# A decoder layer on one core: the first attention stage moved ahead of the memory's keys and values

## The chip, the core and the metric

The kernel runs on one core of a Trainium2 chip. The metric is device time in microseconds (us) of one execution; lower is better. Before the change the median of three runs is 1987.96 us (1984.94 to 2330.19).

The core has a matrix engine (TensorE, PE in the rows, with its weight loads as PEld), VectorE (DVE), ScalarE (ACT), GpSimd (POOL) and SyncE (SP), which in this kernel only issues DMAs. Each engine runs its own instructions in program order and waits on semaphores for the others.

## What is computed

One layer of a decoder with 1024 tokens of width 1024, all in f32:

```python
h = rmsnorm(x, attn_norm)
proj = h @ w_in
qkv_a, b_q, b_k, b_v, m_q = split(proj)
o_a = dilated_mixture_attn(qkv_a, positions)      # A: 3 groups (dilation 1, 4, 16), 4 heads of 64
o_b = sink_swa_gqa(b_q, b_k, b_v, positions)      # B: window 128, 8 query and 2 key heads
o_m = memory_attn(m_q, mem, w_mem_kv)             # M: 4 heads of 128 into 256 memory tokens
merged = sum(sigmoid(h @ w_gate + b_gate) * (o @ w_o)) over the three branches
x = x + merged @ w_out
x = x + conv_ffn(rmsnorm(x, ffn_norm))            # up, causal conv of 3, SwiGLU, down
```

Queries and keys are normalised per head, and in A and B a quarter of the head's dimensions is rotated by angles made from `positions`. The memory's keys and values are `rmsnorm(mem) @ w_mem_kv`.

## The kernel before

The program is four blocks one after the other: `input_projections` (projections and all attention), `gated_outputs`, `output_projection` and `feed_forward`. Only the first is changed.

A product of two f32 matrices is made from three: every operand is split into a high part (a cast by ACT) and a low part (the rest, a subtraction by POOL or DVE), and PE sums hi*hi, hi*lo and lo*hi.

The work of `input_projections` is a list of stages, `STAGES` (line 26). A stage has eight slices of a weight (128 rows each, 512 or 768 columns) and two or eight tiles of 128 tokens. A job is one tile against all eight slices: 24 matmuls of 512 columns (memk, memv, M), with 24 more of 256 columns in A and B. There is one place for the split weights (`w_hi`, `w_lo`), so slice k of the next stage is cast (`cast_slice`, L571) only when the last job of the stage before it has used its slice k; then it is lowered (`w_low`, L351) by POOL for even and by DVE for odd k. Before the split a slice lies raw in one of a few places, some of them in `attn_out`, which is filled with results only later; `raw_slot` gives the place, and SP loads into a place when the slice that it held has been split.

Before the change the stages run as memk, memv, A0, A1, A2, B, M: jobs 0 and 1 are memk, 2 and 3 memv, 4 to 11 A0 (dilation 1), 12 to 19 A1, and so on.

All engines go through slots j = 0, 1, 2, ... In slot j:

- PE projects job j, slice by slice (`project`, L1027 and L1029). After slice 5 it turns the queries and keys of job j-1 (`turn`, L1051).
- ACT, DVE and POOL make them ready before that: ACT squares the projection (L585) and copies values out (L594, L598), DVE sums the squares (L774), POOL takes the root (L488, L490), DVE scales (L798), POOL multiplies by the gains (L499) and rotates (L510 to L515).
- The attention of job j-2 is done in two or four units between the slices (`score`, `turn_probs`, `weigh_values` on PE, `minima` on DVE, `exps` on ACT).

A token tile is prepared by a chain of its own: load, `x_square` (ACT, L559), `x_rms` (POOL, L472 and L473), `x_scale` (DVE, L702), `turn_x` (PE, eight transposes, L998), `x_gain` (DVE, L709), `x_high` (ACT, L539), `x_low` (POOL or DVE, L339). There are ten tiles: numbers 0 and 1 are of the memory and are prepared first, 2 to 9 are of x. The latter come in pairs in slots 0, 2, 4 and 5 (`X_SLOTS`), each at fixed places among the slot's other instructions. Two PSUM areas are shared by the tiles, the turned queries and the scores, so these wait for each other.

SP's queue, in order: the memory tiles, the gains' rows, four weight slices, x tiles 2 and 3, four more slices; then, when slices are split, the other six x tiles; then `load_constants` (positions in three orders, head gains and sinks, 11 small DMAs); then the slices of memv and of all later stages. The angles are made by DVE in slots 1 (`angles`, L714 to L733) and 4 (`reduce_angles`, L743 to L751), the sines by ACT, and the tables by DVE (L759 to L762).

## Time and profile before

| | us |
|---|---|
| median of three runs (1984.94, 1987.96, 2330.19) | 1987.96 |
| span of the profiled execution, first to last instruction | 1979.5 |
| PE busy | 1859.2 (94%) |
| DVE busy | 710.4 (36%) |
| POOL busy | 581.4 (29%) |
| ACT busy | 539.1 (27%) |
| DMA, 90.75 MB | 15.1% of 16 engines' span |

The profiled execution is known by its span alone; the page gives no device time for it. Its span is 5.4 us below the fastest run and 8.5 us below the median, and that difference is what lies around the first and the last instruction, and what one run differs from another. The page's times are from the span's start. A row gives busy time, count and mean of a group of instructions, and the idle time of their engine just before them with what ended it. The granted clock is a share of TensorE's full 2.4 GHz: 1.00 or 0.50, and in between where a stretch holds both.

### The profile page before, as it was taken

How to read it: one execution, taken by the hardware profiler on the slowest of the kernel's cores; microseconds unless marked ns; L12 is line 12 of the kernel's file. 1: busy time of each engine (PE TensorE's matmuls, PEld its weight loads, DVE VectorE, ACT ScalarE, POOL GpSimd, SP SyncE). 2: the span in 40 equal slices, each digit the busy share in tenths (PEclk: the TensorE clock that was granted, in tenths of full speed). 3: DMA queues.
4: the chain of work that ended last, by engine and by line, in shares of the span. 5: the costliest groups of instructions: out<-in, count | busy, mean ns of one | idle time of the engine just before them, and what ended most of it. 6: DMA issues, size and time to landing. Idle time of an engine off the chain costs nothing. (4 is left out here: it accounts for less than half of the span.)

```text
span 1979.5 us, 23310 instructions
## 1 busy us (share of the span) xinstructions
PE 1859.2 (94%) x8777; PEld 1483.2 (75%) x8777; DVE 710.4 (36%) x1318; ACT 539.1 (27%) x1029; POOL 581.4 (29%) x503
## 2 busy tenths in 40 slices
PE   4799999998877979999999989899999999999999
PEld 3577999986665856666666668688888888888887
DVE  4634223235666431111111153242444243424343
ACT  4434223233344431111111142322122212221221
POOL 5445235343232211111111053242133213321321
PEclk8899999998999989999999999899999999999999
DMA  5202002000010042111110060221122102210102
GB/s 197 83 32 65 1 1 64 1 17 14 2 42 1 1 88 54 45 38 35 38 45 24 0 198 1 64 85 32 32 64 64 41 23 64 64 42 21 43 22 85
DMA packets 112818, 90.75 MB, mean 46 GB/s; under 512 B 16812, under 2 KB 97388, under 8 KB 112748
## 3 DMA queue, kind: packets, MB, share of 16 engines
q1 hardware_dynamic: 112748, 89.81, 15.1%
q8 instruction: 44, 0.72, 0.2%
q14 instruction: 26, 0.21, 0.0%
HBM read 85.54 MB, written 4.26 MB: 45 GB/s over the span
## 5 line engine op out<-in xcount | busy, mean ns | idle before, releaser
L1779 PE MATMUL ps<-act_hi,f_hi 128*128 128x512 f32 x704 | 274.7, 390 | 6.3 <-DVE f_lo L1547 6.3
L1779 PE MATMUL ps<-act_lo,f_hi 128*128 128x512 f32 x704 | 274.6, 390 | 0.0
L1779 PE MATMUL ps<-act_hi,f_lo 128*128 128x512 f32 x704 | 274.5, 390 | 0.0
L1547 POOL TENSOR_TENSOR f_lo<-merged,f_hi 128x1024 fp32r<-128x1024 f32 x65 | 156.6, 2438 | 83.7 <-ACT f_hi L1628 83.7
L1320 PE MATMUL ps<-act_hi,g_hi 128*128 128x512 f32 x384 | 170.5, 444 | 3.2 <-DVE g_lo L1303 3.2
L1027 PE MATMUL ps<-w_hi,act_hi 128*128 128x512 f32 x320 | 160.4, 501 | 8.1 <-DVE attn_out L709 4.8
L1779 PEld LDWEIGHTS ps<-act_hi,f_hi 128*128 128x128 f32 x704 | 132.7, 188 | 34.1 <-DVE f_lo L1547 6.6
L1292 DVE TENSOR_TENSOR gate<-ps,gate 128x512 f32<-128x512 f32 x48 | 33.2, 692 | 345.4 <-PE ps L1330 345.4
L1330 PE MATMUL ps<-attn_out,o_w 128*128 128x512 f32 x320 | 148.3, 602 | 6.8 <-ACT o_w L1244 3.2
L1734 DVE TENSOR_TENSOR attn_out<-ps,attn_out 128x512 f32<-128x512 f32 x160 | 106.1, 686 | 134.6 <-PE ps L1799 134.6
L1779 PEld LDWEIGHTS ps<-act_hi,f_lo 128*128 128x128 f32 x704 | 132.6, 188 | 27.6
L1779 PEld LDWEIGHTS ps<-act_lo,f_hi 128*128 128x128 f32 x704 | 132.6, 188 | 27.6
L1276 POOL TENSOR_TENSOR g_lo<-g_raw,g_hi 128x1024 fp32r<-128x1024 f32 x23 | 54.5, 2370 | 330.3 <-ACT g_hi L1239 330.3
L1320 PE MATMUL ps<-act_lo,g_hi 128*128 128x512 f32 x384 | 150.9, 393 | 0.0
L1320 PE MATMUL ps<-act_hi,g_lo 128*128 128x512 f32 x384 | 150.5, 392 | 0.0
L1027 PE MATMUL ps<-w_lo,act_hi 128*128 128x512 f32 x320 | 144.8, 453 | 0.0
L1027 PE MATMUL ps<-w_hi,act_lo 128*128 128x512 f32 x320 | 144.3, 451 | 0.0
L1799 PE MATMUL ps<-f_hi,z_hi 128*128 128x512 f32 x352 | 137.0, 389 | 0.2 <-issue 0.2
L1799 PE MATMUL ps<-f_hi,z_lo 128*128 128x512 f32 x352 | 136.9, 389 | 0.0
L1799 PE MATMUL ps<-f_lo,z_hi 128*128 128x512 f32 x352 | 136.9, 389 | 0.0
L1256 ACT ACTIVATE gate<-ps,gate_bias 128x512 f32<-128x512 f32 x48 | 33.0, 687 | 324.7 <-PE ps L1320 324.6
L1330 PEld LDWEIGHTS ps<-attn_out,o_w 128*128 128x128 f32 x320 | 58.8, 190 | 72.4 <-issue 67.0
(198 smaller groups left out, 3340.0 us busy)
## 6 DMA issues: line engine op xcount, KB each, us to landing
merged<-in_w_up_dram SPq DMA_DIRECT2D x44, 512.0 KB, 4.0
g_raw<-in_w_gate_dram SPq DMA_DIRECT2D x23, 512.0 KB, 3.9
merged<-in_w_down_dram SPq DMA_DIRECT2D x22, 512.0 KB, 3.5
attn_out<-in_x_dram SPq DMA_DIRECT2D x16, 512.0 KB, 5.0
attn_out<-in_w_in_dram SPq DMA_DIRECT2D x20, 384.0 KB, 4.0
w_raw<-in_w_in_dram SPq DMA_DIRECT2D x12, 384.0 KB, 3.3
w_raw<-in_w_out_dram SPq DMA_DIRECT2D x16, 256.0 KB, 3.7
out_dram<-attn_out SPq DMA_DIRECT2D x8, 512.0 KB, 2.6
```

The costliest lines, as they stand in the source:

```text
L1027: ins = pe.matmul(proj_a(j)[:, 0:na], lhs, w[:, k, 0:na], start=(k == 0 and i == 0), stop=(k == 7 and i == 2))
L1256: act.activation(gate[:, u % 2, :], ps[:, 2 * (u % 3), :], ACT.Sigmoid, bias=bias[:, bass.ds(column, 1)]).then_inc(gate_done, 1)
L1276: pool.tensor_tensor(g_lo[:, b], g_raw[:, b], g_hi[:, b].bitcast(F32), ALU.subtract).then_inc(g_lo_done[b], 1)
L1292: dve.tensor_tensor(gate[:, u % 2, :], ps[:, 2 * (u % 3) + 1, :], gate[:, u % 2, :], ALU.mult).then_inc(weighed, 1)
L1320: ins = pe.matmul(ps[:, 2 * (u % 3), :], w[:, b, k, :], a[:, k, cols], start=(k == 0 and i == 0), stop=(k == NK - 1 and i == 2))
L1330: ins = pe.matmul(ps[:, 2 * (u % 3) + 1, :], o_w[:, O_SLOT[b] + i, :], attn_out[:, t0 + i, cols], start=(i == 0), stop=(i == tiles - 1))
L1547: eng.tensor_tensor(f_lo[:, b, :], f_raw[b], f_hi[:, b, :].bitcast(F32), ALU.subtract).then_inc(f_lo_done[b], 1)
L1734: dve.tensor_tensor(dst, ps[:, 4 + i % 4, :], dst, ALU.add).then_inc(y_added, 1)
L1779: ins = pe.matmul(ps[:, 2 * q + half, :], w[:, q, k * P:(k + 1) * P], a[:, k, half * 512:(half + 1) * 512], start=(k == 0 and i == 0), sto ...
L1799: ins = pe.matmul(ps[:, (0 if last else 4) + i % 4, :], z[:, p, t * P:(t + 1) * P], w[:, 4 + p, half * 512:(half + 1) * 512], start=(p == ...
```

## The change

The stage list begins with A0; memk and memv follow, then A1 as before. So jobs 0 to 7 are now A0, 8 and 9 memk, 10 and 11 memv, and from job 12 on nothing moves. Tiles 0 to 7 are now of x, and 8 and 9 of the memory. Tiles 0 and 1 are prepared first, 2 to 5 among the slices of slot 0, 6 to 9 in slot 1. The order is written out by hand on each engine.

The memory's split tiles move to the space of `attn_out`, over x tiles that are done with. A0's and memk's and memv's raw slices have four places each. `load_constants` now comes after x tile 3 and ahead of A0's raw slice 4. The memory tiles are loaded into the places of x tiles 4 and 5, once the tiles up to 6 (for tile 8) and up to 7 (for tile 9) are split. The angles, their reduction, the sines and the tables are made in slots 0 and 1. DVE makes the angles with two multiplications over 192 columns in place of 16 over 24, for which POOL writes eight frequencies. The squares of x tiles go to a buffer of their own. The space reserved for dynamic DMA descriptors is set to 1024 bytes; it makes room in memory, and POOL issues no DMA here.

```diff
 STAGES = [
+    ("A", 0, 0, 0, 512, 256, 8),
     ("memk", 0, 0, 0, 512, 0, 2),
     ("memv", 0, 0, 512, 512, 0, 2),
-    ("A", 0, 0, 0, 512, 256, 8),
     ("A", 1, 1, 768, 512, 256, 8),
     ("A", 2, 2, 1536, 512, 256, 8),
     ("B", 0, 0, 2304, 512, 256, 8),
...
     if n < 8:
-        first, places = 0, (0, 1, 6, 7, 8, 9, 10, 11)
+        first, places = 0, (0, 1, 2, 3)
     elif n < 24:
-        first, places = 8, (0, 1, 2, 3)
+        first, places = 8, (0, 1, 10, 11)
...
-        x_slot = [attn_out[:, n, :] for n in range(NX)]
+        x_slot = [attn_out[:, 2 + n, :] for n in range(8)] + [attn_out[:, 6 + n, :] for n in range(2)]
...
+        def x_place(n):
+
+            return (act_hi, act_lo, n) if n < 8 else (mem_hi, mem_lo, n - 8)
+
+        def x_group(n):
+            return n if n < 2 else 1 + n // 2
...
+            def load_x(n):
+                sp.dma_start(x_slot[n], x_t[n] if n < 8 else mem_t[n - 8]).then_inc(x_in[x_group(n)], 16)
...
+                if n == 0:
+                    load_x(0)
+                    sp.dma_start(gain_rows[0:NK, :], attn_norm[0].rearrange("(k p) -> k p", p=P)).then_inc(gain_in, 16)
+                    sp.dma_start(gain_rows[NK:2 * NK, :], mem_norm[0].rearrange("(k p) -> k p", p=P)).then_inc(gain_in, 16)
+                if n == 1:
+                    load_x(1)
                 if n == 4:
                     load_x(2)
+                    load_x(3)
+                    load_constants()
+                if n == 6:
+                    load_x(4)
+                    load_x(5)
                 if n == 8:
-                    for m in (4, 6, 8):
-                        w_split(sp, m - 2)
-                        w_split(sp, m - 1)
+                    load_x(6)
+                    load_x(7)
+                    for m in (8, 9):
+                        x_split(sp, m - 1)
                         load_x(m)
-                    load_constants()
+                if n == 8 + 2:
+                    x_split(sp, 8)
...
+            freqs = np.exp(np.arange(HALF, dtype=np.float32) * np.float32(-2.0 * math.log(ROPE_THETA) / ROT))
+            for f in range(HALF):
+                link(pool.memset(freq[:, f:f + 1], float(freqs[f])))
...
+            x_rms(0)
+            x_rms(1)
+            x_low(pool, 0)
+            w_low(pool, 0)
+            w_low(pool, 2)
+            x_rms(2)
+            x_rms(3)
+            w_low(pool, 4)
+            x_low(pool, 2)
+            x_rms(4)
+            x_rms(5)
+            w_low(pool, 6)
+            x_low(pool, 4)
+            x_rms(6)
+            x_rms(7)
...
+                if j == 1:
+                    x_low(pool, 6)
+                    x_rms(8)
+                    x_rms(9)
+                    x_low(pool, 8)
...
+            x_square(0)
+            x_square(1)
+            x_high(0)
+            cast_slice(0)
+            x_high(1)
+            cast_slice(1)
+            cast_slice(2)
+            cast_slice(3)
+            x_square(2)
+            x_square(3)
+            cast_slice(4)
+            cast_slice(5)
+            x_high(2)
+            x_high(3)
+            x_square(4)
+            x_square(5)
+            cast_slice(6)
+            cast_slice(7)
+            x_high(4)
+            x_high(5)
+            x_square(6)
+            x_square(7)
+            sines()
...
+                if j == 1:
+                    x_high(6)
+                    x_high(7)
+                    x_square(8)
+                    x_square(9)
+                    x_high(8)
+                    x_high(9)
...
+                for part in range(2):
+                    link(dve.tensor_tensor(angle[:, part, :].rearrange("p (o f) -> p o f", f=HALF),
+                                           pos_f[:].rearrange("p o t -> p (o t)").unsqueeze(2).to_broadcast([P, 24, HALF]),
+                                           freq[:].unsqueeze(1).to_broadcast([P, 24, HALF]), ALU.mult))
...
+            x_scale(0)
+            x_scale(1)
+            x_gain(0)
+            x_gain(1)
+            w_low(dve, 1)
             x_low(dve, 1)
-            for k in range(1, 8, 2):
-                w_low(dve, k)
-            for n in pair_of(0):
-                x_scale(n)
+            w_low(dve, 3)
+            x_scale(2)
+            x_scale(3)
+            w_low(dve, 5)
+            x_gain(2)
+            angles()
+            x_gain(3)
+            x_scale(4)
+            x_scale(5)
+            w_low(dve, 7)
+            x_gain(4)
+            x_low(dve, 3)
+            x_gain(5)
+            x_low(dve, 5)
+            reduce_angles()
+            x_scale(6)
+            x_scale(7)
             n = 0
             for j in range(NJ + LAG + 1):
                 if 0 <= j - 1 < NJ:
                     sum_squares(j - 1)
+                    if j == 1:
+                        rope_tables()
...
+                if j == 1:
+                    x_gain(6)
+                    x_gain(7)
+                    x_low(dve, 7)
+                    x_scale(8)
+                    x_scale(9)
+                    x_gain(8)
+                    x_gain(9)
+                    x_low(dve, 9)
...
                 if k == 0:
                     if kind in ("memk", "memv"):
-                        x_split(pe, 2)
-                    elif s == 2:
-                        x_split(pe, 3 + t)
+                        x_split(pe, NX)
+                    elif s == 0:
+                        x_split(pe, t + 1)
...
+                    if j == 0 and k % 2:
+                        turn_x(2 + k // 2)
+                    if j == 1 and k < 4:
+                        turn_x(6 + k)
                     if k == TURN_AT[0] and 0 <= j - 1 < NJ:
-                        if j <= X_SLOTS[-1]:
-
-                            pe.wait_ge(x_gained, 1 + 2 * sum(slot <= j for slot in X_SLOTS) + (j not in X_SLOTS))
+                        if j == 1:
+                            pe.wait_ge(x_gained, NX)
                         turn(j - 1, 0)
...
-    nc = _bacc.Bacc("TRN2", target_bir_lowering=False, num_devices=1)
+    nc = _bacc.Bacc("TRN2", target_bir_lowering=False, num_devices=1, dynamic_dma_scratch_size=1024)
```

On SP, before: the queue from the last x tile to memv's first slice. `pos_i` are the positions, `gains` the head gains, `w_raw` a raw slice.

```order
L388 DMA attn_out<-in_x_dram 128x1024
L393 DMA pos_i<-in_positions_dram 128x8x1
L395 DMA pos_i<-in_positions_dram 128x4x1 x2
L397 DMA pos_i<-in_positions_dram 128x8
L400 DMA gains<-in_a_q_norm_dram 128x192
L400 DMA gains<-in_a_k_norm_dram 128x192
L400 DMA gains<-in_b_q_norm_dram 128x64
L400 DMA gains<-in_b_k_norm_dram 128x64
L400 DMA gains<-in_m_q_norm_dram 128x128
L400 DMA gains<-in_m_k_norm_dram 128x128
L401 DMA neg_sink<-in_b_sinks_dram 128x8
L440 DMA w_raw<-in_w_mem_kv_dram 128x512
```

On SP, after: the same queue from the last of the small DMAs on (L391, L392), with A0's raw slices 4 to 7 (L442), the x tiles 4 to 7 and the two memory tiles (L379).

```order
L391 DMA gains<-in_m_k_norm_dram 128x128
L392 DMA neg_sink<-in_b_sinks_dram 128x8
L442 DMA w_raw<-in_w_in_dram 128x768
L442 DMA w_raw<-in_w_in_dram 128x768 [waits w_lo_odd]
L379 DMA attn_out<-in_x_dram 128x1024 [waits w_lo_even]
L379 DMA attn_out<-in_x_dram 128x1024
L442 DMA attn_out<-in_w_in_dram 128x768
L442 DMA attn_out<-in_w_in_dram 128x768 [waits w_lo_odd]
L379 DMA attn_out<-in_x_dram 128x1024 [waits w_lo_even]
L379 DMA attn_out<-in_x_dram 128x1024
L379 DMA attn_out<-in_mem_dram 128x1024 [waits x_lo_odd,x_lo_even] x2
L442 DMA w_raw<-in_w_mem_kv_dram 128x512
```

Before, no weight slice of the first stage stood behind the small DMAs; now the slices 4 to 7 do, and the memory tiles wait for low parts.

On DVE, before: its first instructions, up to the first normalised queries and keys.

```order
L702 TENSOR_SCALAR attn_out<-attn_out,row_rstd 128x1024 [waits x_rstd] x2
L709 TENSOR_TENSOR attn_out<-ps,norm_gain 128x1024 [waits gain_ready,x_turned]
L709 TENSOR_TENSOR attn_out<-ps,norm_gain 128x1024 [waits x_turned]
L339 TENSOR_TENSOR mem_lo<-attn_out,mem_hi 128x8x128 [waits x_hi]
L351 TENSOR_TENSOR w_lo<-w_raw,w_hi 128x512 [waits w_hi_done]
L351 TENSOR_TENSOR w_lo<-attn_out,w_hi 128x512 [waits w_hi_done] x3
L702 TENSOR_SCALAR attn_out<-attn_out,row_rstd 128x1024 [waits x_rstd] x2
L709 TENSOR_TENSOR attn_out<-ps,norm_gain 128x1024 [waits x_turned] x2
L339 TENSOR_TENSOR act_lo<-attn_out,act_hi 128x8x128 [waits x_hi]
L774 TENSOR_REDUCE head_ss<-square 128x4 [waits sq_done]
L798 TENSOR_TENSOR qk<-ps,head_rstd 128x512 [waits rstd_done]
```

On DVE, after: from the low part of slice 3 on, in slot 0 (L347 is `w_low`, L724 `x_scale`, L731 `x_gain`, L335 `x_low`).

```order
L347 TENSOR_TENSOR w_lo<-attn_out,w_hi 128x768 [waits w_hi_done]
L724 TENSOR_SCALAR attn_out<-attn_out,row_rstd 128x1024 [waits x_rstd] x2
L347 TENSOR_TENSOR w_lo<-w_raw,w_hi 128x768 [waits w_hi_done]
L731 TENSOR_TENSOR attn_out<-ps,norm_gain 128x1024 [waits x_turned]
L736 TENSOR_SCALAR neg_sink<-neg_sink 128x8 [waits const_in]
L739 TENSOR_REDUCE parity<-prob 128x1 [waits masks_built,dve_chain]
L740 TENSOR_SCALAR parity<-parity 128x1 [waits dve_chain]
L743 TENSOR_SCALAR masks<-masks,parity 128x64 [waits dve_chain] x2
L749 CAST pos_f<-pos_i 128x24 [waits dve_chain]
L751 TENSOR_TENSOR prob<-pos_f,freq 128x192 [waits dve_chain] x2
L731 TENSOR_TENSOR attn_out<-ps,norm_gain 128x1024 [waits x_turned,dve_chain]
L724 TENSOR_SCALAR attn_out<-attn_out,row_rstd 128x1024 [waits x_rstd] x2
```

Before, all eight slices were lowered ahead of the third tile; now the gains of tiles 2 to 5 stand behind the low parts of slices 5 and 7.

## Rows read from the trace of the kernel before

**Rows 1.** Stretches: busy time of each engine, granted clock, DMA share, GB/s.

```profile
core 0: us, PE busy (x) PEld busy (x) DVE busy (x) ACT busy (x) POOL busy (x), PEclk, DMA share, GB/s
0.00:108.00 108.00, 63.80 (x287) 52.15 (x288) 61.85 (x81) 43.88 (x66) 55.25 (x65) 0.83 0.39 129
108.00:185.00 77.00, 75.13 (x515) 61.05 (x514) 25.78 (x79) 32.15 (x85) 35.54 (x51) 1.00 0.11 37
```

**Rows 2.** Who waited for whom, PE, 0 to 110 us: total, times, longest.

```profile
PE ps L1051 <- POOL qk L499: 9.5, 1, 9.5
```

**Rows 3.** Timeline of ACT: squares after A0's jobs 1 and 7.

```profile
107.73 0.60 ACT L585 ACTIVATE square<-ps 128x512 f32<-128x512 f32 x1 [3.46 <-PE ps L1029]
...
185.94 0.59 ACT L585 ACTIVATE square<-ps 128x512 f32<-128x512 f32 x1
```

**Rows 4.** Timeline of SP, 20 to 36 us, and the first cast behind it.

```profile
20.54 4.17 SPq L388 DMA_DIRECT2D attn_out<-in_x_dram  x6
24.75 0.53 SPq L393 DMA_DIRECT2D pos_i<-in_positions_dram  x1
25.32 4.14 SPq L395 DMA_DIRECT2D pos_i<-in_positions_dram  x2
...
32.01 0.43 SPq L400 DMA_DIRECT2D gains<-in_a_q_norm_dram  x1
...
35.34 0.91 SPq L440 DMA_DIRECT2D w_raw<-in_w_mem_kv_dram  x2
...
43.03 1.29 ACT L571 ACTIVATE w_hi<-w_raw 128x512 fp32r<-128x512 f32 x2 [7.37 <-DMA w_raw<-in_w_mem_kv_dram]
```

**Rows 5.** DMA issues, 0 to 120 us: KB each, median us to landing.

```profile
attn_out<-in_w_in_dram SPq DMA_DIRECT2D x8, 384.0 KB, 4.6
...
attn_out<-in_mem_dram SPq DMA_DIRECT2D x2, 512.0 KB, 4.0
```

**Rows 6.** Timeline, one tile's chain: the first tile.

```profile
6.35 1.05 ACT L559 ACTIVATE square<-attn_out 128x1024 bf16<-128x1024 f32 x1
...
8.43 0.75 DVE L702 TENSOR_SCALAR attn_out<-attn_out,row_rstd 128x1024 f32<-128x1024 f32 x1 [8.43 <-POOL row_rstd L473]
...
11.25 1.23 DVE L709 TENSOR_TENSOR attn_out<-ps,norm_gain 128x1024 f32<-128x1024 f32 x1 [0.59 <-PE ps L998]
...
13.64 2.35 POOL L339 TENSOR_TENSOR mem_lo<-attn_out,mem_hi 128x1024 fp32r<-128x1024 f32 x1 [3.77 <-ACT mem_hi L539]
```

**Rows 7.** Groups by shape, 0 to 110 us: slices of 768 columns, and the cast.

```profile
L351 POOL TENSOR_TENSOR w_lo<-w_raw,w_hi 128x768 fp32r<-128x768 f32 x2 | 3.7, 1851 | 2.0 <-ACT w_hi L571 2.0
L571 ACT ACTIVATE w_hi<-w_raw 128x768 fp32r<-128x768 f32 x4 | 3.3, 838 | 5.7 <-DMA w_raw<-in_w_in_dram 5.7
...
L351 DVE TENSOR_TENSOR w_lo<-attn_out,w_hi 128x768 fp32r<-128x768 f32 x2 | 2.7, 1352 | 1.0 <-ACT w_hi L571 1.0
```

**Rows 8.** Timeline: DVE's small multiplications, its reduction of the angles; one job's POOL chain.

```profile
53.50 3.56 DVE L733 TENSOR_SCALAR prob<-pos_f 128x24 f32<-128x24 f32 x16
...
90.28 0.25 DVE L743 TENSOR_SCALAR prob_t<-prob 128x192 f32<-128x192 f32 x1
...
93.63 0.36 DVE L751 TENSOR_SCALAR prob<-prob 128x384 f32<-128x384 f32 x1
...
96.54 0.20 POOL L488 TENSOR_SCALAR head_rstd<-head_ss 128x8 f32<-128x8 f32 x1 [7.26 <-DVE head_ss L774]
...
102.21 0.45 POOL L515 TENSOR_TENSOR qk<-rope_a,rope_b 128x128 f32<-128x128 f32 x1
```

**Rows 9.** Timeline of PE: two matmuls' starts at the lower clock, two at the full.

```profile
90.40 0.63 PE L1027 MATMUL ps<-w_lo,act_hi 128*128 128x512 f32 x1
...
91.04 0.63 PE L1027 MATMUL ps<-w_hi,act_lo 128*128 128x512 f32 x1
...
92.00 0.39 PE L1027 MATMUL ps<-w_lo,act_hi 128*128 128x512 f32 x1
...
92.35 0.39 PE L1027 MATMUL ps<-w_hi,act_lo 128*128 128x512 f32 x1
```

More of the change, by code:

```diff
@@ L80, in raw_group @@
 def raw_group(n):
-    place = raw_slot(n)
-    if n < 8:
-        return n
-    return place if place < 4 else 2 + place % 4
+    return {0: 0, 1: 1, 2: 2, 3: 3, 4: 2, 6: 3, 8: 6, 9: 7, 10: 4, 11: 5}[raw_slot(n)]
 def raw_before(n):
@@ L163, in layer @@
         half_power = sb("half_power", [P, 16])
+        with ExitStack() as early:
+            sb("below_mem", [P, 2, S], ctx=early)
+            mem_hi = sb("mem_hi", [P, NK, 256], F32R, ctx=early)
+            mem_lo = sb("mem_lo", [P, NK, 256], F32R, ctx=early)
         attn_out = sb("attn_out", [P, 10, S])
@@ L237, in input_projections @@
         stats = sb("stats", [P, 3, 8, 8])
-        with ExitStack() as early:
-            mem_hi = early.enter_context(nc.sbuf_tensor("mem_hi", [P, NK, 256], F32R))
-            mem_lo = early.enter_context(nc.sbuf_tensor("mem_lo", [P, NK, 256], F32R))
         q_ring = sb("q_ring", [P, RQ, 4, P])
@@ L261, in input_projections @@
                  (("max", 32), ("e", 96), ("total", 32), ("f", 96))}
-        mem_in = [sem(f"mem_in{n}") for n in range(2)]
-        x_in = [sem(f"x_in{n}") for n in range(4)]
+        x_in = [sem(f"x_in{n}") for n in range(6)]
         const_in = sem("const_in")
@@ L355, in v_wait @@
         def v_wait(eng, j):
-            before = units_before(j - RK + 2)
+            writer = [i for i in range(j) if KIND[i] in V_KINDS and KIND[i] != "memv" and i % RK == j % RK]
+            before = units_before(writer[-1] + 2) if writer else 0
             if before:
@@ L474, in x_rms @@
                                    ALU.pow).then_inc(x_rstd, 1)
-            for n in (0, 1):
-                x_rms(n)
-            x_low(pool, 0)
             def norm_and_rope(j):
@@ L537, in x_high @@
                 act.wait_ge(x_gained, n + 1)
[L538 removed]
+                hi, _, c = x_place(n)
+                if n == 8:
+                    x_split(act, 4)
                 act.activation(hi[:, :, c * P:(c + 1) * P], x_slot[n].rearrange("p (k n) -> p k n", n=P),
@@ L582, in squares @@
                         act.wait_ge(factor_turned, spreads)
-                    if j <= X_SLOTS[-1]:
-                        act.wait_ge(x_sq, 2 + 2 * sum(slot <= j + 1 for slot in X_SLOTS))
                     ins = act.activation(square[:, 0:512], proj_a(j), ACT.Square)
@@ L654, in _ @@
             act.activation(norm_gain[:].rearrange("p a k -> p (a k)"), ps[:, OB, 0:2 * NK], ACT.Copy).then_inc(gain_ready, 1)
-            for n in (0, 1):
-                x_square(n)
-            for n in (0, 1):
-                x_high(n)
-            for k in range(8):
-                cast_slice(k)
-            for n in pair_of(0):
-                x_square(n)
+            x_square(0)
[21 more added lines that the diff above has]
+            sines()
             n = 0
@@ L666, in _ @@
                     squares(j - 1)
-                for m in pair_of(j + 1):
-                    x_square(m)
+                if j == 1:
[5 more added lines that the diff above has]
+                    x_high(9)
                 for k in range(8):
@@ L674, in _ @@
                         n += 1
-                    if k == 4:
-                        for m in pair_of(j):
-                            x_high(m)
                     if k == TURN_AT[0] and 0 <= j - 1 < NJ:
@@ L971, in _ @@
                         merge_use(MERGE_AT.index((j, k)))
-                if j == 1:
-                    angles()
-                if j == 4:
-                    reduce_angles()
-                    rope_tables()
                 if j == merge_from:
@@ L991, in turn_x @@
                     pe.wait_ge(x_gained, n - 1)
-                    keys = count(HAS_K, slot_of_x(n) - 1)
-                    if keys:
-                        pe.wait_ge(k_done, keys)
                 elif n == 1:
```

69 lines of the change are left out of this document (10 added, 59 removed).

## The prediction

> **What bounds the kernel now.** I read the page first: PE is busy for 1859.2 of 1979.5 us, so the change can win only where PE is idle or runs at the lower clock, in the part that it touches. The stretches come next. In the first 108 us PE is busy for 63.8 us at a granted clock of 0.83; in the next 77 us, which are A0's jobs 2 to 7, it is busy for 75.1 us at 1.00 [rows 1]. So 44 us of idle time lie ahead of 108 us, and hardly 2 us behind. The other engines are no bound there either: DVE, the busiest, has 61.9 us of work in 108 [rows 1]. What binds is the chain that prepares tiles and slices. The waits name its worst place: 9.5 us for the first queries and keys, which had to wait on POOL for the gains [rows 2]. The timeline of SP shows why the gains were late. The small DMAs were issued from 24.75 us on, behind six x tiles; SP was not rid of them until 35.34; and a slice issued right behind them was cast only at 43.03, 7.7 us later [rows 4].
>
> The landmark for the sum is the end of A0's job 1. Before, it is 107.7 us, with the four memory jobs already done [rows 3].
>
> **The change, part by part.** I follow the new order with the durations of the rows; times are from the span's start.
>
> *To the first matmul.* The first tile's chain is the same, only that the tile is of x. Its square began at 6.35 and its low part ended at 13.64 + 2.35 = 16.0 [rows 6]. The squares' own start should be 0.5 us earlier, since one DMA less stands ahead of the gains' rows: low part at 15.5. POOL then lowers slice 0, now 768 columns, 1.85 us [rows 7]: 17.3. Before, the first slice was lowered at 18.2. So one us is won here.
>
> *Slices 4 to 7.* SP's queue holds back tiles 2 and 3 until slice 0 is lowered, 17.4. Issuing two tiles takes 0.9, and the eleven small DMAs follow at 18.3. Before, they took SP from 24.75 to 35.34, 10.6 us [rows 4], partly because six tiles stood ahead of them; at 0.5 us each, as those from 32.01 on, they would take 5.5. So raw slice 4 is issued between 23.7 and 29, and I take 27: two tiles are a third of six, but the small pieces are as many. It lands 7.7 us later as behind the same DMAs before [rows 4], at about 35. The lower bound is 23.7 + 4.6, the landing time of a slice of 384 KB [rows 5], so 28.3; the upper is 29 + 7.7 = 37.
>
> The Trainium skill prices such a load otherwise. DMA: Bandwidth & Descriptors, section "Anatomy of one DMA — SWDGE (gpsimd) path", has 2.0 us plus the bytes over 436 GB/s, fitted on the other issuing path: 2.9 us for 384 KB. The row with 7.7 us for a smaller slice disagrees as long as small pieces stand ahead. By the rule the slice would land at 29.9, and the sum below would be some 5 us less.
>
> *Slot 0.* DVE lowers slice 5 ahead of the gain of tile 2, and ACT casts slices 4 and 5 ahead of the high part of tile 2. So both engines stand still from about 25.6, when tile 3 is scaled, until slices 4 and 5 have landed: cast at 37, lowered at 38.2. All that follows is in series. Gain of tile 2 (1.22) 39.4; the angles, 2.2 (some 1.4 for the small steps ahead, which stay, and two multiplications of 192 columns at 0.35 each, as the widest of rows 8, in place of sixteen that took 3.56 [rows 8]) 41.6; gain of tile 3 42.8; its high part 43.9; squares of 4 and 5 (1.2 each) 46.3; root and scale of 5, 48.0; POOL and DVE lower slices 6 and 7, 49.2. PE runs slices 6 and 7 at the lower clock, because it was mostly idle before: 1.95 us each, three pairs at 0.64, where the full clock needs three at 0.35 [rows 9]; then it turns tile 5, 54.7. Gain 56, high part 57, low part 58.3.
>
> *Slot 1.* The reduction of the angles takes DVE 3.7 us [rows 8]: 62. It stands ahead of the scales of tiles 6 and 7, which PE needs for its turns after slices 0 and 1: 63.5. Then sum of squares, tables and roots, and the normalised queries at 66.9. POOL's gains and rotation take 3.4 us (the chain of [rows 8], 96.54 to 102.66, is 6.1; the root and DVE's scaling are its first 2.7), the low part of tile 6 2.35 [rows 6]: 72.8. Only then may SP load memory tile 8, because it goes into tile 4's place under a wait for the low parts of tiles up to 6. It takes 4.0 us [rows 5], 77; square, root and scale as the first tile's 2.1 plus 0.75 [rows 6], 79.9. PE waits for this from about 70 on; queued behind the turn of tile 8 are the rest of job 1 and the queries of job 0. Turn, slice 3 and turn of tile 9 at the lower clock: 85.2. The last four slices and `turn` at the full clock: 4.8. **A0's job 1 ends at 90.**
>
> *The memory jobs.* Their PE work now stands behind A0: 4 jobs of 24 matmuls at 0.233 (two thirds of 0.35, rows 9), 22.5, and 0.7 for two turns. Stalls are new. In slot 8 the queries of A0's last job need 7.6 us from squares to rotation (1.4 and then the 6.1 of rows 8), and a short job gives them 4.2 us and two units of attention: 1 us lost, and 0.4 in slot 9. In slot 10 memk's last keys need 5 us and start behind ACT's casts, with 4.2 us of cover and no units: 3.6. Together 5. The bounds are 0, if the casts are early, and 20, a job's 5.6 us lost at each of four slots less the overlap. I take 5 as the stalls follow from rows.
>
> *A0's jobs 2 to 7* took 78.2 us [rows 3]. Now 1.1 less: no start at the lower clock, and narrower slices to cast in the last one. From job 12 on the order is that of before; units of attention are the same in number, so what moves out of slots 12 and 13 moves into 8 and 9.
>
> *Costed at nothing:* eight small writes by POOL (over before the first square lands, at most 2 us), the squares' own buffer, the descriptor space, the table loads of ACT (it is idle when each comes).
>
> **The sum.** 90 + 22.5 + 0.7 + 5 - 1.1 - 107.7 = +9.4. The profiled span of 1979.5 becomes 1988.9; with the 8.5 us by which the median lies above the span, 1997.4.
>
> **The rivals.**
>
> *1. The loads hold nothing up.* Slice 4 lands at its lower bound, 28.3 instead of 35 (-6.7), and the memory jobs do not stall (-5): -2.3, 1986. For it: SP's delay before came behind 3 MB of tiles. Against it: the 7.7 us from the issue at 35.34, when the tiles had long gone. The page's rule named above belongs here.
>
> *2. Preparation runs at DVE's speed.* Ten tiles need 10 x (0.75 + 1.22) + 5 x 1.8 (between a gain's 1.2 and POOL's 2.35), four slices 5.4, the angles and tables 7: 41 us of DVE. If it is hardly ever kept waiting, job 1 ends near 8 + 41 + 15 = 64, and the time is 26 us less than forecast: 1971. For it: each tile's steps are interleaved with another's. Against it: in-order engines with a load between them; before, DVE was busy for little more than half of 108 us [rows 1].
>
> *3. Four places for raw slices are too few.* This is the other side, clearly slower than before. memk, memv and A1's start take 24 slices through few places: each group of four waits for cast and low part (2.7) and a load (4.6) [rows 5, 7], 7.3 us for four slices, where PE needs 2.8 at the full clock in a memory job. If this is not hidden behind slots 7 to 9, four groups lose 4.5 each: +18, 2015. It decides if the loads start only when the slot before has ended. Against it: slot 7 lasts 13 us and its casts start early.
>
> **How the numbers follow.** Forecast 0.50, rival 1 0.22, rival 2 0.13, rival 3 0.15. The range takes in rivals 1 and 2's time as its lower end and nearly rival 3's as its upper: 1970 to 2014. About 2% (40 us) is what a measurement of this kernel can tell from no change. To be faster by that, nearly all of the 44 us of idle time would have to go: 0.02. Slower by that needs rival 3 twice over: 0.02. Within 2%: 0.96.
>
> **What would show it.** Right: ACT idle before the cast of slice 4 until 33 to 37 us; PE idle for 8 us or more before slice 4 in slot 0 and again before the turn of the first memory tile; squares after job 1 at 86 to 94; granted clock near 0.5 to 60 us; a wait of 3 us or more before memk's last turn. Wrong: job 1 over before 80, or slice 4 cast before 30; and if PE waits in the memory slots for `w_lo`, rival 3 holds.

## The result, and where the profile puts it

| | us | ratio to before, 95% interval |
|---|---|---|
| before, run beside it | 1987.34 (median of 4) | |
| after | 2000.89 (median of 4; 1996.87 to 2005.06) | 1.0081 [1.0057, 1.0105] |
| forecast | 1997.4, range 1970 to 2014 | |
| span of after's profiled execution | 1995.1 (before 1979.5) | |

Slower by 0.8% in the ratio, which leaves out the one slow execution of before, of 2330.19 us; the two medians alone give 0.7%. That is well inside the 2% of the prediction, but the interval does not reach 1. The stretches come first. This is the changed kernel over the stretches of [rows 1].

```profile
core 0: us, PE busy (x) PEld busy (x) DVE busy (x) ACT busy (x) POOL busy (x), PEclk, DMA share, GB/s
0.00:108.00 108.00, 59.14 (x295) 49.43 (x295) 50.87 (x71) 39.39 (x65) 46.09 (x75) 0.83 0.28 92
```

PE is busy for 59.1 us instead of 63.8. No other engine filled up: DVE fell from 61.9 to 50.9. So it is waiting, not work. The mean clock reads 0.83 as before, but it can't be compared: the row has 1.00 for the first stretch of matmuls, and these took 0.63 us, the time at the lower clock in [rows 9].

```profile
17.00:24.00 7.00, 4.18 (x12) 3.22 (x12) 4.88 (x3) 1.89 (x4) 3.11 (x3) 1.00 0.66 157
```

```profile
18.36 0.63 PE L1057 MATMUL ps<-w_lo,act_hi 128*128 128x512 f32 x1
```

The waits of PE over the first 215 us, up to the first jobs of A1, say for whom it waited.

```profile
engine line waited for: us in total, times, longest us
PE ps L1028 <- DVE attn_out L724: 35.3, 6, 12.8
PE ps L1057 <- POOL w_lo L347: 8.8, 3, 4.6
PE ps L1019 <- DMA square<-in_mem_norm_dram: 4.8, 1, 4.8
PE ps L1081 <- POOL qk L500: 3.0, 1, 3.0
PE ps L1081 <- issue: 2.0, 2, 1.6
PE ps L1121 <- issue: 1.2, 1, 1.2
PE ps L1135 <- ACT prob_t L645: 1.0, 1, 1.0
```

L1028 is `turn_x`, and DVE's L724 is `x_scale`. The 9.5 us of [rows 2] behind POOL's gains are gone. In their place stand 35.3 us behind the scaling of token tiles, in six turns, and 3.0 us (L1081) in slot 10. The largest piece is shown by the timeline of after: the small DMAs with slice 4 behind them, its cast, then slot 1 with the loads of the memory tiles, the first memory tile's square, PE's turn, and the squares after job 1.

```profile
18.30 0.43 SPq L384 DMA_DIRECT2D pos_i<-in_positions_dram  x1
18.78 1.35 SPq L386 DMA_DIRECT2D pos_i<-in_positions_dram  x2
20.17 2.13 SPq L388 DMA_DIRECT2D pos_i<-in_positions_dram  x1
22.35 0.43 SPq L391 DMA_DIRECT2D gains<-in_a_q_norm_dram  x1
...
25.67 0.91 SPq L442 DMA_DIRECT2D w_raw<-in_w_in_dram  x2
...
32.35 0.84 ACT L580 ACTIVATE w_hi<-w_raw 128x768 fp32r<-128x768 f32 x1 [7.38 <-DMA w_raw<-in_w_in_dram]
...
71.87 1.46 SPq L379 DMA_DIRECT2D attn_out<-in_mem_dram  x2
...
78.30 1.06 ACT L568 ACTIVATE squares_junk<-attn_out 128x1024 bf16<-128x1024 f32 x1 [8.56 <-DMA attn_out<-in_mem_dram]
...
81.20 1.97 PE L1028 MATMUL ps<-ident,attn_out 128*128 128x128 f32 x8 [12.75 <-DVE attn_out L724]
...
90.25 0.60 ACT L592 ACTIVATE square<-ps 128x512 f32<-128x512 f32 x1 [1.73 <-PE ps L1059]
```

Slice 4 was issued at 25.67 and could be cast only at 32.35; all of slot 0 stands behind it. The first memory tile was issued at 71.87, as SP had to wait until tile 6 was split, and PE stood for 12.75 us before its turn. Job 1 ended at 90.25; forecast was 90.

The load itself was not what took until 78.30. The two memory tiles share one semaphore (`x_group` in the diff), and `x_square` waits until both have landed. The first landed 3.4 us after its issue, at 75.3; the second was issued only at 73.0 and landed 5.3 us later:

```profile
attn_out<-in_mem_dram SPq DMA_DIRECT2D x1, 512.0 KB, 3.4
attn_out<-in_mem_dram SPq DMA_DIRECT2D x1, 512.0 KB, 5.3
```

So 3.0 us pass between the landing of the first tile and its square. The second was issued late because SP waited for tile 7's low part, and that took DVE 3.15 us beside POOL's low part of tile 6. Tile 3's, with POOL idle, had taken 1.21.

```profile
69.50 2.34 POOL L335 TENSOR_TENSOR act_lo<-attn_out,act_hi 128x1024 fp32r<-128x1024 f32 x1
69.77 3.15 DVE L335 TENSOR_TENSOR act_lo<-attn_out,act_hi 128x1024 fp32r<-128x1024 f32 x1 [1.12 <-ACT act_hi L554]
```

No experiment gave the two tiles a semaphore each, so what that would save is not shown.

To follow the difference further I use the squares that ACT takes after a job as landmarks, in each kernel. Before, those after A0's job 1, A0's job 7 and the stages' job 15 (an A1 job, with everything moved already done) were at 107.73, 185.94 and 247.21; after, at 90.25, 166.95 and 259.79. So at job 15 the changed kernel is 12.6 us behind. From there on both run the same instructions, and yet the spans end 15.6 apart. 3.0 us arise in code that did not change. Experiment 11 looks for where.

### The profile page after: what moved, and what is told of

It reads as the page before. It is cut to its first block and busy times, and to the rows that moved or that the text cites. A ratio compares the mean times of both kernels' runs of the same rounds, so it can differ in the third digit from the quotient of the medians.

```text
span 1995.1 us, 23306 instructions
## 1 busy us (share of the span) xinstructions
PE 1862.3 (93%) x8777; PEld 1485.1 (74%) x8777; DVE 710.9 (36%) x1304; ACT 538.9 (27%) x1029; POOL 578.7 (29%) x511
```

## The experiments

Each ratio is against the kernel before, timed beside it on the same chip; the experiments used four chips. "Job 1" is A0's, "job 15" the landmark above; these and the span come from one profiled execution each. That execution was the slowest of ten in experiment 2, and the fastest of four, 7 us below the median, in experiment 6. So where a landmark and a ratio differ by a few us, the ratio is the surer one.

| | job 1 | job 15 | span | ratio, 95% interval |
|---|---|---|---|---|
| before | 107.73 | 247.21 | 1979.5 | 1 |
| after | 90.25 | 259.79 | 1995.1 | 1.0081 [1.0057, 1.0105] |
| 1 small DMAs late | 83.10 | 253.82 | 1988.8 | 1.0042 [1.0025, 1.0059] |
| 2 memory tiles in an own place | 85.16 | 256.13 | 1995.2 | 1.0036 [1.0024, 1.0048] |
| 3 both | 76.03 | 248.30 | 1981.4 | 1.0001 [0.9985, 1.0016] |
| 4 as 2, six raw places | 83.92 | 253.27 | 1990.1 | 1.0037 [1.0021, 1.0054] |
| 5 before, small DMAs early | 105.98 | 245.58 | 1981.0 | 0.9987 [0.9977, 0.9997] |
| 6 after, small DMAs early | 82.26 | 252.24 | 1986.7 | 1.0057 [1.0039, 1.0075] |
| 7 as 3, slot 1 reordered | 76.67 | 246.18 | 1982.0 | 1.0006 [0.9995, 1.0018] |
| 8 as 7, small DMAs and angles early | 76.53 | 247.45 | 1984.6 | 0.9997 [0.9987, 1.0007] |
| 9 angles through slot 0 | 70.78 | 240.33 | 1973.3 | 0.9991 [0.9979, 1.0002] |
| 10 as 9, memv's last casts behind the squares | 69.91 | 239.82 | 1972.9 | 0.9976 [0.9968, 0.9985] |
| 11 after, unchanged | 90.86 | 260.41 | 1995.4 | 1.0084 [1.0068, 1.0100] |
| 12 after, memv's last casts behind the squares | 91.72 | 261.78 | 1997.0 | 1.0073 [1.0056, 1.0091] |

### 1. The small DMAs late

```diff
                     load_x(3)
-                    load_constants()
...
                     load_x(7)
+                    load_constants()
...
             x_gain(2)
-            angles()
             x_gain(3)
...
             x_low(dve, 5)
+            angles()
             reduce_angles()
```

> Theory: raw slice 4 was cast at 32.4 us because it stood behind the eleven small DMAs on SP, and DVE stood still for it. With the small DMAs behind x tile 7 (and the angles made just ahead of their reduction) slice 4 is cast by 25, tile 3's gain starts near 31.5 instead of 41.2, and the angles' 4 us come later in the chain: A0's job 1 ends near 84.5 instead of 90.3, time 6 us less than the changed kernel. Rival (the slot is bound by DVE's and ACT's own work): job 1 ends within 2 us of 90. Rival (the memory tiles' load hides it): the wait ahead of the first memory tile grows from 12.8 us by what is won before.

The cast of slice 4 and DVE's two multiplications of the angles, in this kernel:

```profile
24.63 1.56 ACT L580 ACTIVATE w_hi<-w_raw 128x768 fp32r<-128x768 f32 x2
...
49.36 0.75 DVE L751 TENSOR_TENSOR prob<-pos_f,freq 128x192 f32<-128x192 f32 x2
```

The cast comes 7.7 us earlier (32.35 in after), job 1 ends 7.15 earlier, and job 15 is 6.0 earlier. The edit moves two things, though: the angles' multiplications left their place beside POOL's low part too, and took 0.75 us where they had taken 2.77. Experiment 6 moves the small DMAs alone. PE's wait for the first memory tile is still 11.8 us.

### 2. The memory tiles in a place of their own

```diff
+        mem_raw = sb("mem_raw", [P, 2, NK * P])
...
-        x_slot = [attn_out[:, 2 + n, :] for n in range(8)] + [attn_out[:, 6 + n, :] for n in range(2)]
+        x_slot = [attn_out[:, 2 + n, :] for n in range(8)] + [mem_raw[:, n, :] for n in range(2)]
...
                     for m in (8, 9):
-                        x_split(sp, m - 1)
                         load_x(m)
```

> Theory: PE's 12.8 us ahead of the first memory tile are the load that may only start after the low parts of tiles 4 to 7. With a buffer of their own the memory tiles are loaded by 42 us; DVE scales the first of them right after tile 7's low part, near 73.5 instead of 80.4, and job 1 ends near 83: 7 us less than the changed kernel. Rival (DVE's order binds, not the load): the scale moves by less than 2 us and the time by less than 2.

PE's wait for the first memory tile falls from 12.8 to 6.2 us, job 1 ends 5.1 earlier and job 15 3.7 earlier. The other 6 us of the wait are not the load. The tile's square stands on ACT behind the high parts of tiles 6 and 7, and these behind gains that DVE makes only after the queries of job 0.

The 1.4 us that are lost between job 1 and job 15 lie in slot 8: from the squares after job 7 to those after job 8 it is 12.8 us here and 11.4 in after. PE's idle pieces ahead of it were 1.3 and 1.0 us long, as in after, and the granted clock fell here, not there:

```profile
168.00:172.00 4.00, 3.04 (x18) 2.11 (x15) 1.15 (x5) 2.68 (x8) 1.58 (x5) 0.67 0.00 0
```

The timed runs show more than the landmark, 1.0036 against after's 1.0081.

### 3. Both

> Both edits. Theory (two places of one serial chain): the gains add up, job 1 ends near 77, 13 us less than the changed kernel, level with the kernel before. Rival (they cover each other): no more than the larger of the two, 7 us.

Job 1 ends 14.2 us earlier, more than the two parts' sum of 12.2: they don't hide each other. But of 14.2 only 11.5 are left at job 15, 2.7 less. The stretches show where they went, around the idle piece in slot 10, first in this kernel and then in after, where the slot lies some 14 us later.

```profile
176.00:186.00 10.00, 6.58 (x26) 5.25 (x27) 5.05 (x5) 2.09 (x5) 5.47 (x5) 0.85 0.69 229
186.00:192.00 6.00, 6.00 (x20) 4.77 (x19) 1.03 (x1) 3.35 (x5) 2.10 (x2) 0.68 0.04 14
```

```profile
192.00:198.00 6.00, 3.06 (x14) 2.21 (x12) 3.26 (x4) 0.40 (x1) 3.88 (x4) 1.00 0.83 267
198.00:204.00 6.00, 5.93 (x28) 4.99 (x29) 2.17 (x2) 3.69 (x6) 2.18 (x3) 1.00 0.32 126
```

PE waits 3.0 us for the same keys in both. After that wait the granted clock fell to its lower level for some microseconds in experiment 3 (0.68 as the mean of six us), and in after it stayed at 1.00. The landmarks show the price: from the squares after job 9 to those after job 12 it is 28.6 us here and 25.8 in after.

### 4. Six places for raw slices

```diff
     elif n < 24:
-        first, places = 8, (0, 1, 10, 11)
+        first, places = 8, (0, 1, 10, 11, 8, 9)
```

This kernel also holds the edit of experiment 2.

> The memory tiles' own buffer, and six places for raw slices in memk and memv in place of four. Theory (memory jobs stall on the short job's cover, not on loads): same as the own buffer alone, within 1 us. Rival 3 of the prediction (too few places): PE's idle time in the memory slots, 8 us, goes down by 3 us or more.

Against experiment 2: from job 1 to job 15 169.35 instead of 170.97, the wait in slot 10 is 2.9 instead of 3.0, and the ratio is the same. Of the 1.6 us, 0.7 are won before the memory jobs start, and in after no wait of PE for `w_hi` or `w_lo` stands in the memory slots. Rival 3 of the prediction falls: the four places cost between nothing and 1.6 us, where it needed 18.

### 5. The small DMAs early, in the kernel before

```diff
+                if n == 8:
+                    load_constants()
                 if raw_before(n) is not None:
...
-                    load_constants()
```

> The kernel before, with its eleven small DMAs issued right after the first eight slices, at about 8 us, in place of behind the six x tiles. Theory (small pieces on SP's queue cost whatever is queued behind them, in either order of stages): the gains are there before 30 us, PE's 9.5 us ahead of the first turn shrink to 6 or less, memv's first slice is cast before 36 instead of 43, and the time is 4 to 8 us less than before. Rival (before was bound elsewhere in its first 108 us): within 2 us of before.

PE's waits for DVE and POOL in L1052 (`turn`), 0 to 215 us, where [rows 2] had 9.5:

```profile
PE ps L1052 <- DVE attn_out L710: 7.8, 1, 7.8
...
PE ps L1052 <- POOL qk L500: 5.6, 1, 5.6
```

The wait falls by 3.9 us, but job 1 comes only 1.75 earlier and job 15 1.6; 4 to 8 were expected. Of the 3.9 us, 1.5 are lost ahead of it: the squares of the first memory job come at 31.81, before at 30.27. Another 0.5 go to the next wait, that for the gained x tiles (L710), 7.8 us here and 7.3 before. In the span even the rest is gone: it is 1.5 us longer, because 2.5 us appear near 735 us and 0.6 later, in code that is the same. The ratio says that the gain is small; its interval just excludes 1.

### 6. The small DMAs early, in the changed kernel

They stand right behind A0's raw slice 3, on SP from 4.2 to 13.6 us; the angles stay where they were.

> The changed kernel with only the place of the small DMAs moved, to right after raw slice 3, at about 4 us, while SP would wait for slice 0. Angles stay in slot 0. Theory: slice 4 is cast by 25 as in the run with the small DMAs behind tile 7, tile 3's gain starts near 36 (the angles are ahead of it again), job 1 ends 5 to 7 us before the changed kernel's 90.3, time 6 us less. Rival (they delay the first tile or the first slices): low part of slice 0 ends later than 18.5 and the gain is below 3.

Slice 4 is cast at 24.06, job 1 ends 8.0 earlier and job 15 7.5. This agrees with experiment 1 from the other side. What counts is not that the small DMAs are late, but that they don't stand ahead of a load for which all wait. The timed runs show less than the profile: 1.0057 against after's 1.0081 is some 5 us. The angles' two multiplications took 2.85 us here as in after 2.77, against 0.75 in experiment 1.

### 7. Slot 1 reordered

On top of both: squares, roots and scales of the memory tiles, and the gains of tiles 6 and 7, stand ahead of the angles.

> Both edits of e_both, and slot 1 in another order: squares, roots and scales of the memory tiles and the gains of tiles 6 and 7 ahead of the angles, the low parts behind. Theory (in-order engines wait in slot 1 for tiles that are ready): job 1 ends near 70 instead of 76, 6 us less than e_both. Rival (DVE's own work binds slot 1 now): within 2 us of e_both.

```profile
PE ps L1081 <- POOL qk L516: 11.8, 1, 11.8
```

A miss. The wait for memory tiles is gone, and PE waits 11.8 us for the turned queries of job 0 instead. DVE's reduction now ends at 61.6 instead of 53.4, behind the memory tiles' scales and two gains; ACT's sines wait for them, and the squares of job 0 stand behind the sines, at 62.09 where experiment 3 had 53.82. Job 1 ends where it did.

### 8. The same with small DMAs and angles early

> e_best with the small DMAs right after raw slice 3 and the angles ahead of tile 2's scale, where DVE has been idle. Theory: 3 us less than e_best, job 1 ends near 67, and 8 us or more less than the kernel before. Rival (the small DMAs are not there by 22 us): DVE waits for them ahead of tile 2, and all that follows is late by that.

A miss too. The wait is 9.6 instead of 11.8, and the squares of job 0 come at 61.98: it was the reduction and the sines, not the angles, that held them.

### 9. The angles spread through slot 0

With the small DMAs early, the memory tiles' own place and their squares, roots and scales as in experiment 7: angles ahead of the scale of tile 2, reduction behind the gain of tile 3, sines behind the cast of slice 7, tables ahead of tile 5's low part. The order of DVE, cut:

```diff
             w_low(dve, 3)
+            angles()
             x_scale(2)
             x_scale(3)
             w_low(dve, 5)
             x_gain(2)
-            angles()
             x_gain(3)
+            reduce_angles()
             x_scale(4)
...
             x_gain(5)
+            rope_tables()
             x_low(dve, 5)
-            reduce_angles()
```

> The two last runs moved PE's wait from the memory tiles to the first turn (11.8 and 9.6 us behind POOL's rotation), because the squares of job 0 stand behind the sines. Here the angles stand ahead of tile 2's scale, their reduction behind tile 3's gain, the sines behind slice 7's cast and the tables ahead of tile 5's low part, all places where the engine waited, and slot 1 begins with the squares. Theory: squares of job 0 near 52 instead of 62, job 1 ends near 65, 11 us less than e_best and 8 to 12 us less than the kernel before, ratio near 0.995. Rival (DVE has no idle time left in slot 0): tile 5's gain is late by what was moved, ratio 0.999 or more.

```profile
PE ps L1028 <- DVE attn_out L725: 16.6, 5, 4.4
PE ps L1081 <- POOL qk L517: 4.7, 1, 4.7
```

The squares of job 0 come at 52.16, the wait falls to 4.7 us, and job 1 ends 5.9 earlier than in experiment 7. The 35.3 us of after, 12.8 of them in one piece, are now 16.6 in pieces of at most 4.4. Job 15 is 6.9 us ahead of before and the span 6.2 shorter. The timed runs show less of it: 0.9991, and the interval holds 1.

### 10. memv's last two casts behind the squares of memk's last job

```diff
                 if 0 <= j - 1 < NJ:
                     squares(j - 1)
+                if j == 10:
+                    cast_slice(22)
+                    cast_slice(23)
...
-                    if j in last_job_of.values() and JOBS[j][0] + 1 < len(STAGES):
+                    if j in last_job_of.values() and JOBS[j][0] + 1 < len(STAGES) and not (j == 9 and k > 5):
                         cast_slice(
```

The low parts of the two slices move behind the sums and the root of that job in the same way. The rest is experiment 9.

> The same, and in slot 9 memv's slices 6 and 7 are cast behind the squares of memk's last job, slice 7 is lowered behind DVE's sum, slice 6 between POOL's root and gains. Theory (that turn is late because ACT, DVE and POOL are on the next weights): its wait of 3.0 us falls to about 1.5, squares of that job come 1.5 us earlier after the slot's end, 1 to 3 us less than e_slot0, more where the granted clock had fallen in slot 10. Rival (the slices 6 and 7 are then late themselves): PE waits for w_lo instead, no gain.

The wait in slot 10 falls from 2.8 to 1.9 us. Job 15 is only 0.5 us ahead of experiment 9, since from job 7 to job 8, ahead of the edit, it takes 12.8 us instead of 11.1, at a lower clock as in experiment 2. With 1977.36 against 1981.88 this kernel is faster than before, 0.9976 [0.9968, 0.9985], and the only version of the new order of which that is shown. Its interval overlaps with that of experiment 9, so the edit's own worth is not shown.

### 11. The changed kernel again

> The changed kernel, untouched: what repeats in it and what does not. Theory A (the 13.5 us by which it was slower than before lie in the new start: 12.6 us at the landmark, the rest is scatter of the unchanged 1735 us that follow): squares after job 15 again at 259.8 within 0.5 us, span less that landmark anywhere from 1732 to 1739, ratio to before between 1.005 and 1.008. Rival B (something in the later stages was made slower too): the landmark the same, and span less landmark again 3 us above the 1732.3 of before or more, the ratio 1.008 or above.

The ratio is 1.0084, as B said. Span less landmark is 1735.0 (after 1735.3, before 1732.3). That is 2.7 above before, just short of B's 3, and inside A's bounds too. So the number repeats within this kernel. But the same unchanged code takes 1733.0 to 1739.1 us in the profiles of the eleven other experiments, and 1735.4 in experiment 5, whose order is that of before. Before's own profile, of which there is only one, is the lowest of fourteen. That the 3 us belong to the new order is not shown.

Where they lie can be read. The difference between the matched instructions does not grow evenly: it steps by 0.6 near 730 us and by 1.5 near 1255, where `feed_forward` begins. There eight transposes are followed by the same idle time in each kernel. The timelines of before, and then of after:

```profile
1247.61 1.09 PE L1476 MATMUL ps<-ident,merged 128*128 128x128 f32 x8 [2.42 <-DVE merged L1461]
...
1255.03 0.79 PE L1779 MATMUL ps<-act_hi,f_hi 128*128 128x512 f32 x1 [6.32 <-DVE f_lo L1547]
...
1258.18 0.63 PE L1779 MATMUL ps<-act_lo,f_hi 128*128 128x512 f32 x1
1258.60 0.56 PE L1779 MATMUL ps<-act_hi,f_lo 128*128 128x512 f32 x1
1259.00 0.40 PE L1779 MATMUL ps<-act_hi,f_hi 128*128 128x512 f32 x1
```

```profile
1261.78 1.97 PE L1507 MATMUL ps<-ident,merged 128*128 128x128 f32 x8 [2.42 <-DVE merged L1492]
...
1270.06 0.79 PE L1810 MATMUL ps<-act_hi,f_hi 128*128 128x512 f32 x1 [6.31 <-DVE f_lo L1578]
...
1274.49 0.63 PE L1810 MATMUL ps<-act_lo,f_hi 128*128 128x512 f32 x1
1274.92 0.58 PE L1810 MATMUL ps<-act_hi,f_lo 128*128 128x512 f32 x1
1275.34 0.39 PE L1810 MATMUL ps<-act_hi,f_hi 128*128 128x512 f32 x1
```

The transposes take 0.9 us more in after, at the lower clock already. Then, before, the matmuls run at the lower clock's 0.63 for 3.6 us after PE has resumed; after, for 4.9, which costs another 0.6. The same work, some 15 us later, meets the lower level over a longer part of it. So this step of 1.5 us, half of the 3, is shown to be the clock. In experiments 4, 5 and 9 the eight transposes take 1.09 to 1.29 us, in 1, 2, 3, 6, 7, 8, 11 and 12 they take 1.69 to 1.97. The steps near 730 us and between 1100 and 1200 stay unexplained.

### 12. The wait in slot 10 alone

The edit of experiment 10, in the changed kernel.

> The changed kernel with only memv's slices 6 and 7 cast and lowered behind the squares, sums and root of memk's last job. It prices the stall in slot 10 (3.0 us) alone, with the start left slow. Theory A (slot 10 waits for the head's chain because the casts and the low parts stand ahead of its squares): PE's wait for the gained keys there falls from 3.0 to 1.9 us or less and the landmark after job 15 comes 1 to 2 us earlier than in the unchanged kernel; ratio about 0.001 lower. Rival B (what is won is lost again in slot 11, where the casts then end later): the wait falls, slot 11 gains a wait for w_hi or w_lo of 1 us or more, and the landmark is where it was within 0.5 us.

PE's wait in slot 10, and the stretch that follows it in this kernel:

```profile
PE ps L1088 <- POOL qk L502: 2.1, 1, 2.1
```

```profile
198.00:204.00 6.00, 5.53 (x19) 4.58 (x20) 0.69 (x1) 1.70 (x3) 0.59 (x2) 0.72 0.51 171
```

Neither theory. The wait falls from 3.0 to 2.1 as A said, no wait for `w_hi` or `w_lo` appears, and yet job 15 comes 1.4 us later than in experiment 11. Of this 0.9 is there at job 1 already, ahead of the edit, and is scatter (the same code has 90.25 and 90.86 there). Where PE resumes in slot 10 the granted clock is 0.72, at 1.00 in after, and from job 9 to job 12 it takes 27.5 us instead of 25.8. A shorter wait was followed by the lower clock, the longer one not. The ratios, 1.0073 and 1.0084, cannot be told apart.

## Why the prediction was right, and where its sum was off

**The forecast case came:** slower, within the range, and for the main reason given. Its sign came from one comparison. A0's start ends 17.5 us earlier than before (90.25 against 107.73), but the four memory jobs, which were part of that time, are still to be paid. Step by step:

- *To the first matmul*: 17.58 (forecast 17.3).
- *Slices 4 to 7*: issued at 25.67 (27; bounds 23.7 and 29), landed and cast from 32.35 on (35; lower bound 28.3). The landing took 6.7 us from the issue, 1 less than the 7.7 that I took from [rows 4]. The Trainium skill, in DMA: Bandwidth & Descriptors, section "Anatomy of one DMA — SWDGE (gpsimd) path", has a fit for the other issuing path; by it the landing would take an estimated 2.9. The trace disagrees by 3.8 us, and by 2.0 and 2.2 in experiments 1 and 6, where no small pieces stand directly ahead (4.9 and 5.1). Experiments 1 and 6 show the 6 to 8 us that this place costs. Most of it is SP's time for issuing: 7.4 us, from 18.30 to 25.67.
- *Slot 0*: slice 5 was lowered at 35.9 (38.2), and these 2.3 us were lost again. The angles took 2.8 us for the two multiplications (0.7 forecast), beside POOL's low part, so the gain of tile 3 was done at 42.4 (42.8). The reduction was done at 61.3 (62).
- *Slot 1*: low part of tile 6 done at 71.84 (72.8). The first memory tile's square came 6.4 us after the issue (4.0 forecast). I had it wait for its own load, which took 3.4; it waited for the second tile's too, which the forecast left out. Scaled at about 81, 79.9 forecast. **Job 1: 90.25, 90 forecast.** It is close because terms of opposite sign cancel, not because each was right.
- *A0's jobs 2 to 7*: 76.7 (77.1).
- *The memory jobs*: this is **the step that was mis-sized, the "Stalls are new" term of 5 us**. From the squares after A0's last job to those after job 15 it takes 92.84 us, before 61.27, from 185.94 [rows 3] on. That is 31.6 more, where 22.5 + 0.7 + 5 = 28.2 were forecast. PE's idle pieces between these two ends sum to 7.7 us, 0.5 before; so 7.2 are new where I had 5. In slot 10 it is 3.0 (3.6), in slot 8 1.2 and 1.0 (1), in slot 9 1.6 and 0.5 (0.4), then 0.4 more (none). The excess is mainly the 1.6 ahead of a `turn`, with nothing that the trace shows as its cause. PE's busy time grew by 24.3 where I had 23.2. That leaves 0.1 of rounding.
- *The rest of the program*: "from job 12 on the order is that of before" was true, and I costed it at 0; in the profiles it took 3.0 us more, of which experiment 11 puts 1.5 down to the clock. Whether the new order causes it is open. The median stood 5.8 us over the profiled span instead of 8.5, which hid most of it: 1995.1 + 5.8 against 1988.9 + 8.5.
- *The signs*: squares after job 1 within 86 to 94, PE's wait of 12.75 us before the first memory tile's turn, and the 3.0 us before memk's last turn came. Three did not quite. ACT's idle time ended at 32.35, not at 33 to 37. PE's idle time before slice 4 came in two pieces of 3.7 us, not as 8. And the clock was not low throughout to 60 us: the matmuls took the full clock's 0.39 from 30.0 on, and the row's 0.50 returned for 36.3 to 53.4.

**Rival 1** falls on both halves: slice 4 did not land at 28.3, and the memory jobs did stall. **Rival 2** (preparation at DVE's speed, job 1 near 64) falls for this kernel, but experiments 9 and 10 came to 70.8 and 69.9 with the same work, mainly in another order. So most of the way from 90 to 64 was open to a better order; that 64 itself can be reached is not shown. **Rival 3** is refuted by experiment 4.

**What the new order costs and why it can win.** At job 15 the changed kernel is 12.6 us behind. The small DMAs ahead of slice 4 (6 us alone) and the memory tiles' wait for a place (3.7 alone) made 11.5 of these together. The rest of the start was mostly the order in slots 0 and 1, on DVE above all: 5.3 us at job 1 from experiment 3 to 9. At job 15 the two are 8.0 apart, but 2.8 of these are the lower clock that experiment 3 met in slot 10.

What stays open: that the landmark gains of experiments 9 and 10, 6.9 and 7.4 us, appear as only 1.4 and 4.5 us in the timed runs' medians. One execution is profiled, and the same kernel's timed executions lie 7 to 11 us apart, so I can't say whether that is more than scatter.

## What to carry to other kernels

Reordering stages moves the first stage's costs, it does not remove them; before counting a win, add up what the stage that goes first no longer hides and what the stage that goes later still costs. On an in-order queue, look at what stands directly ahead of the one load that all engines wait for: the position of eleven DMAs of 2 to 96 KB was worth 6 to 8 us at the landmarks here, and 5 to 8 in the timed runs. Look also at what a semaphore counts: tiles that share one wait for the last of them. And when one wait is removed, name the next one on the same path first: experiment 5 shortened its wait by 3.9 us and kept 1.75, and experiment 7 removed its wait and found one of 11.8 us behind it.

## What the runs showed of the hardware that I had not expected

- Small pieces on the queue delay the landing of what is issued right behind them, besides the time that SP needs to issue them. Slice 4, 384 KB, landed 6.7 us after its issue behind them, and 4.9 and 5.1 us after it in experiments 1 and 6, where it stood behind two x tiles. The rows are of after and the two experiments:

```profile
w_raw<-in_w_in_dram SPq DMA_DIRECT2D x1, 384.0 KB, 6.7
w_raw<-in_w_in_dram SPq DMA_DIRECT2D x1, 384.0 KB, 4.9
w_raw<-in_w_in_dram SPq DMA_DIRECT2D x1, 384.0 KB, 5.1
```

- Two multiplications of DVE over 128x192, both inputs from SBUF, took 2.77 and 2.85 us together while POOL subtracted over 128x1024, and 0.75 in experiments 1 and 10, where POOL had only single columns to work on. In after they ended 0.6 us after POOL's subtraction, and the low part of tile 7 above 1.1 us after POOL's: each time about as long after it as the DVE work takes alone. These are the two rows of after:

```profile
38.19 2.35 POOL L335 TENSOR_TENSOR act_lo<-attn_out,act_hi 128x1024 fp32r<-128x1024 f32 x1 [3.12 <-ACT act_hi L554]
...
38.39 2.77 DVE L751 TENSOR_TENSOR prob<-pos_f,freq 128x192 f32<-128x192 f32 x2
```

- A wait of PE of 2 to 3 us was followed by the lower clock in some kernels (experiments 1, 3, 8 and 12: 27.2, 28.6, 27.4 and 27.5 us from job 9 to job 12) and not in others (after, experiments 2, 4, 6, 7, 9, 10 and 11: 25.8 to 25.9), and the wait was no longer in the first group. The stretch took 1.4 to 2.8 us more, up to as much as the wait itself. In experiments 2 and 10 the clock had fallen in slot 8 instead, behind idle pieces of no more than 1.3 us, for 1.4 to 1.7 us. What decides it the runs don't show.
- The same instructions behind the same idle time of 6.3 us got the full clock back after 3.6 us in one kernel and after 4.9 in the other, and the transposes ahead took 1.09 and 1.97 us. So a stretch that nobody touched can take 1.5 us more or less, a thousand us behind the edit. That the edit's shift in time is what changes it is likely, since the changed kernel did it twice, but is not shown.
